# Four weight sums per pair of output chunks: from adding transfers to VectorE, in the last stage of a two-layer trunk step

## What is computed

```
for l in range(2):
    h = rmsnorm(x, norm_pre[l]) * (1 + scale) + shift
    proj = h @ w_in[l]                       # 5120 columns
    ... attention and Fourier mixing (l = 0), pooling and spatial gating (l = 1) ...
    x = x + gate * rmsnorm(o @ w_out[l], norm_post[l])    # o: 384 x 2048, w_out[l]: 2048 x 2048
```

## Time and profile before

| | |
|---|---|
| median of 3 runs | 1118.3 us (1118.1 to 1118.55) |
| the profiled execution | 1118.51 us |
| its span in the trace | 1116.7 us |
| TensorE busy (share of the span) | 1085.9 us (97%) |
| VectorE busy | 747.7 us (67%) |
| ScalarE busy | 462.6 us (41%) |
| GpSimd busy | 60.6 us (5%) |
| adding transfers, L1093 | 32 of 512 KB, median 9.2 us from issue to landing |
| last stage, first matmul of the first pair to the end of the span | 970.1 to 1116.7 us |

### The profile page before, as it was taken

How to read it: one execution, slowest core, us unless ns; L and a number is a source line. 1 busy time by engine, 2 the same in 40 slices (tenths; PEclk the granted TensorE clock), 3 DMA queues, 4 the chain that set the end, 5 groups by cost and what they waited for, 6 DMA issues and landing times.

```text
span 1116.7 us, 13705 instructions
## 1 busy us (share of the span) xinstructions
PE 1085.9 (97%) x5308; PEld 871.5 (78%) x5308; DVE 747.7 (67%) x1077; ACT 462.6 (41%) x747; POOL 60.6 (5%) x98
## 2 busy tenths in 40 slices
PE   6999999999999999999999999999999999999895
PEld 5576687887878878888887888888888888877784
DVE  4555565766776786799957646478656665377657
ACT  4343244434545432343356843222434223366553
POOL 1000010000000000000010000000000000112130
PEclk9999999999999999999999999999999999999998
DMA  9998766455455567577893335355644655579895
GB/s 383 415 401 337 319 238 262 152 227 194 183 225 219 188 256 301 227 274 289 284 358 115 113 114 207 113 201 183 237 157 154 224 193 207 138 177 223 255 230 156
DMA packets 43360, 254.87 MB, mean 228 GB/s; under 512 B 5232, under 2 KB 5344, under 8 KB 17952
## 3 DMA queue, kind: packets, MB, share of 16 engines
q1 hardware_dynamic: 28656, 186.66, 43.5%
q0 software_dynamic: 11952, 63.07, 19.4%
q10 hardware_dynamic: 2688, 4.26, 1.3%
HBM read 250.26 MB, written 3.72 MB: 227 GB/s over the span
## 4 chain that ended last, share of the span: by engine, by line
PE 88%; DVE 4%; DMA 3%; ACT 2%; issue 1%; DVEq 0%; POOL 0%; ACTq 0%; POOLq 0%
PE bank L1218 23%; PE bank L1220 22%; PE bank L1219 22%; PE bank L1166 2%; PE bank L1281 2%; PE bank L1167 2%; PE bank L1168 2%; PE bank L1363 2%; DMA raw_first<-in_ada_first 1%; DMA raw<-in_w_out 1%; PE bank L1302 1%; PE bank L1427 1%; PE bank L1379 1%; PE bank L1342 1%; DVE w_lo L1823 1%
## 5 line engine op out<-in xcount | busy, mean ns | idle before, releaser
L1218 PE MATMUL bank<-w_hi,h_op 128*128 128x512 f32 x1036 | 419.4, 405 | 2.4 <-DVE h_op L2077 2.0
L1220 PE MATMUL bank<-w_hi,h_op 128*128 128x512 f32 x1036 | 405.1, 391 | 0.0
L1219 PE MATMUL bank<-w_lo,h_op 128*128 128x512 f32 x1036 | 404.2, 390 | 0.0
L1823 DVE TENSOR_TENSOR w_lo<-raw,w_hi 128x1024 fp32r<-128x1024 f32 x210 | 256.1, 1222 | 156.1 <-ACT w_hi L1477 155.3
L1477 ACT ACTIVATE w_hi<-raw 128x1024 fp32r<-128x1024 f32 x210 | 219.8, 1056 | 193.3 <-PE bank L1220 162.7
L1218 PEld LDWEIGHTS bank<-w_hi,h_op 128*128 128x128 f32 x1036 | 194.7, 188 | 55.1 <-issue 15.6
L1220 PEld LDWEIGHTS bank<-w_hi,h_op 128*128 128x128 f32 x1036 | 194.4, 188 | 42.0
L1219 PEld LDWEIGHTS bank<-w_lo,h_op 128*128 128x128 f32 x1036 | 195.0, 188 | 36.5
L1827 DVE SCALAR_TENSOR_TENSOR dot_raw<-dot_raw,cond_sb 128x2048 f32<-128x2048 f32 x32 | 73.0, 2280 | 0.0
L1655 ACT ACTIVATE probs_t<-bank 128x384 f32<-128x384 f32 (+1 forms) x36 | 15.1, 420 | 83.1 <-PE bank L1386 83.1
L1166 PE MATMUL bank<-w_hi,h_op 128*128 128x512 f32 x84 | 34.1, 405 | 7.9 <-DVE w_lo L1823 6.6
(11 more groups left out here) (277 smaller groups left out, 1274.5 us busy)
## 6 DMA issues: line engine op xcount, KB each, us to landing
raw<-in_w_in SPq DMA_DIRECT2D x68, 1024.0 KB, 5.0
dot_raw<-in_ada_tiles POOLq DMA_DIRECT2D x32, 1024.0 KB, 5.1
raw<-in_w_out SPq DMA_DIRECT2D x28, 1024.0 KB, 6.7
raw_first<-in_ada_first SPq DMA_DIRECT2D x21, 1024.0 KB, 11.5
raw<-in_ada_groups SPq DMA_DIRECT2D x16, 1024.0 KB, 6.7
raw<-in_ada_halves SPq DMA_DIRECT2D x16, 1024.0 KB, 4.8
raw<-in_w_out POOLq DMA_DIRECT2D x32, 512.0 KB, 9.2
open_raw<-in_w_in SPq DMA_DIRECT2D x24, 512.0 KB, 12.6
```

The lines of the kernel that those rows point to most:

```text
L1218: pe.matmul(out, operand(layer, kind, 0, k, t), hi, start=k == begin, stop=False)
L1219: pe.matmul(out, operand(layer, kind, 0, k, t), lo, start=False, stop=False)
L1220: last = pe.matmul(out, operand(layer, kind, 1, k, t), hi, start=False, stop=k == end)
L1823: dve.tensor_tensor(lo, src, hi.bitcast(F32), ALU.subtract).then_inc(lo_ready, 1)
```

## The change

In `add_weights` the t2 case is taken out, so GpSimd issues t1, then t4 and t3: 12 adding transfers per pair. VectorE forms t2 itself, in place, from the loaded b22: `raw(b11's place) += raw(b22's place)`, 128 x 1024 float32, four times per pair, once per u. A new entry `sum` stands in the timetable at steps 17, 21, 25 and 29 of each pair, ahead of everything else at that step. The sum waits for b22's load and for the split of t1's piece, both through semaphores; the rounding of a t2 piece waits for the new semaphore `t2_summed`. The count on `grown_a` is renumbered to two per pair.

```diff
@@ timetable
     for p, (c, _) in enumerate(PAIRS):
+        for u in range(UPS):
+            put(c, 17 + 4 * u, "sum", p, u)
         for i, n in ((3, 0), (4, 1), (5, 2), (20, 3)):
             put(c, i, "pair_gate", p, n)
@@ wait_pair_source
             elif op == "t3":
                 eng.wait_ge(grown_c[u], 16 * (p + 1))
+            elif op == "t2":
+                eng.wait_ge(t2_summed, UPS * p + u + 1)
             else:
-                eng.wait_ge(grown_a[u], 16 * (3 * p + ("t1", "t2", "t4").index(op) + 1))
+                eng.wait_ge(grown_a[u], 16 * (2 * p + ("t1", "t4").index(op) + 1))
@@ gpsimd
             def add_weights(p, op, u):
-                source, side, low = {"t1": ("b11", 1, 0), "t2": ("t1", 1, HALF_KT), "t3": ("b22", 1, 0),
-                                     "t4": ("t2", 0, HALF_KT)}[op]
+                source, side, low = {"t1": ("b11", 1, 0), "t3": ("b22", 1, 0), "t4": ("t2", 0, HALF_KT)}[op]
...
             for p in range(len(PAIRS)):
-                for op in ("t1", "t2"):
-                    for u in range(UPS):
-                        add_weights(p, op, u)
+                for u in range(UPS):
+                    add_weights(p, "t1", u)
                 for u in range(UPS):
                     add_weights(p, "t4", u)
                     add_weights(p, "t3", u)
@@ vector
+                elif what == "sum":
+                    p, u = e[1:]
+                    wait_pair_source(dve, p, "b22", u)
+                    dve.wait_ge(lo_ready, pair_half(p, "t1", u) + 1)
+                    grown = pair_source(p, "t2", u)
+                    dve.tensor_tensor(grown, grown, pair_source(p, "b22", u), ALU.add).then_inc(t2_summed, 1)
```

More of the change, by code:

```diff
@@ L768, in hybrid_step @@
         taken = sem("taken")
+        t2_summed = sem("t2_summed")
         combined_full = sem("combined_full")
```

## The result

The changed kernel takes 1120.17 us (median of 14 runs, 1119.04 to 1122.8), the kernel before 1118.28 us (14 runs, 1117.6 to 1118.89): a ratio of 1.0021 with a 95% interval of 1.0013 to 1.0029, some 2 us slower. The forecast was 1.5 us faster, and the time lies above the range's upper end of 1119.3. The profiled execution took 1120.29 us with a span of 1118.5, 1.8 us more than before.

What follows compares the result with a forecast made beforehand. TensorE's products plus waits, chiefly for the first pair's last adding transfer, were taken to bound the kernel; 2.6 us earlier there, 1.5 surviving W's keep, second pair 0, gave 1117.0 profiled, 1116.8 median; range 1115.6 to 1119.3.

Steps and rivals of the forecast that it cites:

- what binds: First pair's last adding transfer holds up piece 26 (2.97 us stall); b21's second load limits W's keep in the second pair.
- the sums in the first pair: First two VectorE sums delay TensorE around pieces 12 and 13 by 1.14 + 0.9 = 2.0 us.
- the term of the transfers taken out: First pair: without t2's transfers the last adding transfer lands at 1032.0 instead of 1034.4, if b11's load keeps away.
- the upper bound of 1034.6: Latest landing of the first pair's last adding transfer, if the two delays return in full (2.5 us).
- the overlap of 2.5: b11's load for the second pair delays the first pair's last two adding transfers by 0.9 + 1.6 us.
- the slack: The 4.7 us lost at piece 26 in the old stall and clock absorb TensorE's 2.0 to 3.7 us delay.
- nothing is gained: Rival, 0.28: 1118.3 us; last transfer lands at 1034.4 or later, or waits around piece 12 lower the clock.
- The rule of the Trainium skill: Transfer engines round-robin between queues, so b11's load shares from its issue; overlap returns in full and the transfer gain is nothing.
- The second pair: Four sums, 4.6 us of VectorE, are covered by a 3.5 us lead ahead of piece 12: 0 on the path.
- slower: Rival, 0.10: second pair's sums are not covered and hold up splits and TensorE by 1.14 us each; 1121.4 us.
- The end of the kernel beside TensorE: From piece 19's end on, the chain of joins, takes and residual on VectorE and ScalarE changes by 0.
- The clock: Forecast: stays up behind piece 26. In rival "nothing is gained", waits around piece 12 lower it, costing 1.7 us.

Runs made afterwards that it cites:

- kernels with the later load: b11's first load of the second pair issued behind piece 24's split, not 22's: in the changed kernel 1117.68 us, in the kernel before 1115.73 us.
- first pair alone: Changed kernel with VectorE forming t2 in the first pair only, the second pair keeping its t2 transfers: 1120.83 us, ratio 1.0023.
- idle sums: Kernel before with all transfers, plus two unused half-size VectorE additions at the place of each sum: 1120.68 us, ratio 1.0020.
- after with the later load: Changed kernel with b11's first load of the second pair issued behind piece 24's split instead of piece 22's: 1117.68 us, ratio 0.9994.
- sums behind the splits: Changed kernel with its second, third and fourth sums one step later, behind the splits of pieces 13, 15 and 17: 1120.92 us, ratio 1.0022.
- sums in the second pair alone: Changed kernel with VectorE forming t2 in the second pair only, the first pair keeping its t2 transfers: 1118.14 us, ratio 1.0000.
- without t2: Changed kernel with t2 formed in neither pair, by neither transfers nor VectorE: 1117.19 us, ratio 0.9991.

## Why the prediction was wrong

**Right: what binds.** The last adding transfer behind piece 26, and the kept W of the second pair behind b21's load as the gate through which any gain has to pass. The table shows the second for every kernel with the load in its old place.

**Right: the sums in the first pair.** Predicted 1.4 and 0.9 us ahead of pieces 12 and 13 and TensorE 2.0 us late; measured 1.40 and 0.63, and 2.1 late at piece 24. The first wait grew by 1.13 us, the length of one sum.

**Wrong: the term of the transfers taken out.** The step was "Seven more at 2.48 give 1032.0, if the load of b11 keeps out of their way". The last landing was 1036.3, beyond the upper bound of 1034.6 as well. The 2.4 us by which I had it earlier than the old 1034.4 are the overlap of 2.5, put at nothing; the 1.0 us of latency that I credited to the transfers taken out went against the first issue's 1.15. From the latencies after, issue to landing: the first at 1009.31 + 5.7 = 1015.0, the second at 1011.57 + 6.0 = 1017.6, the third at 1012.99 + 8.3 = 1021.3, the seventh at 1021.15 + 10.8 = 1031.95, the last at 1036.3. The 4.3 us over the forecast are 0.35 on the first landing, 1.2 between the second and the third (3.7 instead of 2.48), 2.6 on the last two (3.15 and 4.35), and 0.2 spread over the rest. The 2.6 is the overlap with the load of b11, which I had priced right at 2.5 and then left out of the forecast. It came back because load and transfers move together: both wait for splits that follow TensorE. The kernels with the later load show its worth directly: 2.5 and 2.8 us of time, and landings 2.9 to 3.0 us earlier. The 1.2 near the start goes with VectorE's additions. In the four kernels that have them ahead of the splits of the first pair (after, first pair alone, idle sums, after with the later load), the second of the eight is issued 2.3 us behind the first instead of 1.1, and the third landed 3.4 to 4.5 us behind the second; in the eight kernels without them, 2.5 us. With the sums behind the splits the third is the first that is issued late, and the fourth landed 3.5 us behind it. Each time it is the transfer behind the late one; why that one takes longer, no run shows.

**Wrong with it: the slack.** I let the old stall of 4.7 us absorb TensorE's delay, on the ground that the last landing was set by the stream's start and its rate. That ground held, but the start stands behind the sums as well. The first of the eight transfers waits for the split of piece 12, the second for that of 13, the third for that of 14. I moved the first issue alone, by 1.15 us. It moved by 1.2, and the second and the third by 2.4: 1011.57 and 1012.99 instead of 1009.22 and 1010.60. The third landed at 1021.3 instead of 1019.5, and the last is as late as that, 1.9 us. So what was to be absorbed had moved the thing it was to be absorbed by. The last transfer's own issue is not the way it went, though it moved most, from 1019.07 to 1022.0: the stream was 1.8 us late before that issue, and with the sums behind the splits a still later issue had an earlier landing. The load of b11 moved along, from 1024.7 to 1026.8, as the prediction had it, and so met the last two transfers as before. The bound of 1034.6 had the overlap returning in full; what it lacks, and the rival "nothing is gained" with it, is the stream's start, 0.35 and 1.2 us.

**The rule of the Trainium skill**, "DMA: Bandwidth & Descriptors", section "SWDGE vs HWDGE vs iDMA", round-robin between queues, had the overlap returning in full, and it did. But how the load started is as in the earlier trace rows: issued at 1026.8, with 246 GB/s moved between 1028 and 1032 and 320 between 1030 and 1034. So the outcome bears the rule's result out, not its immediate sharing. The load issued at 1028.62, behind piece 23, did not slow the last adding transfer either.

**The second pair** was right: no wait of TensorE for a split from piece 12 to 19, and the sums in the second pair alone cost 0.0 us. The rival "slower", put there with 4.6 us, named the wrong pair. The end of the kernel beside TensorE was right too: the last wait ahead of piece 26 of the second pair is 2.06 us instead of 2.08.

**The clock** was not in the way. With the sums in the first pair alone, or without t2, it stayed up behind piece 26; with the sums in the second pair alone it fell, as in the kernel before. The relation of the table held either way: what TensorE lost by it, it would have waited for at the kept W.

**Small slips in the prediction's working**, which change nothing in its outcome: from 1041.2 to 1038.5 it is 2.7 us, not 2.6; 1029.47 + 2.27 + 2.0 is 1033.7; and before 1100 us TensorE has one more wait, of 0.63 us at 1097.03.

## What to carry to other kernels

When a stall is to absorb a delay, follow what ends the stall back to what sets its time. Here that is a queue of eight transfers, and its first three wait for the delayed engine: the stall moved along and absorbed nothing. The issue of the last one decides little while seven lie ahead of it. Before taking transfers out to speed up others, look at what else is in flight when the late one is: here a load that could be issued 4 to 6 us later cost 2.5 to 3.5 us, while the eight transfers taken out gave 0.9 (with an interval from nothing to 2), and nothing that could be measured once the load was out of the way. Work put on an engine that is idle for 33% of the kernel held up TensorE by its full length where that engine was the chain, and by nothing in the second pair; ask for the busy share of the 20 us at hand.

## What the hardware did that was not expected

An adding transfer with the same seven ahead of it, issued at 1019.1 +- 0.1, took 15.3, 14.06 and 13.96 us in three executions. GpSimd's addition of 128 x 1024 float32 takes 2.39 us in the one row in which no VectorE operation with two inputs in SBUF was under way at its start, and 3.25 in the three others, against VectorE's 1.22. VectorE's operations of that kind beside it last 2.2 to 3.4 us and end 1.1 us behind it. And the granted clock does not follow the length of a wait alone. In the changed kernel it fell to 1.2 GHz behind the wait of 2.75 us, where the chain that ended last has products 0.43 us long (start, us, what):

```profile
1039.49 0.43 PE bank L1170
```

With the sums in the second pair alone it fell behind a wait of only 1.78 us (granted clock 0.67 between 1035 and 1040). With the sums in the first pair alone it stayed at 2.4 GHz behind a wait of 3.15 us, by the busy times of the stretch (columns as in the earlier trace rows, the granted clock is the third number from the end):

```profile
1038.00:1043.00 5.00, 3.93 (x17) 3.22 (x18) 5.00 (x5) 3.21 (x4) 1.14 (x2) 1.00 0.59 215
```

Near the end the two kernels differ as well: behind the wait of 2.08 us the granted clock was 0.75 between 1100 and 1105 in the kernel before, behind that of 2.06 us it was 1.00 between 1104 and 1109 in the changed one.
